# A hybrid block on one core: constants, modulation, norm, gates, lead and mixers in one program instead of six

## The reference

```python
c_act = silu(c)
mod = c_act @ ada_w + ada_b                       # 6 parts of 1024
sh_mix, sc_mix, gt_mix, sh_ffn, sc_ffn, gt_ffn = split(mod, 6)
h = rmsnorm(x, norm_mix) * (1 + sc_mix) + sh_mix
proj = h @ w_in                                   # all heads' q, k, v, gates
y = sum over branches sigmoid(merge_b) * mixer_b  # GLA 4 heads, mLSTM 4 heads, gated DeltaNet 8 heads
x = x + gt_mix * (y @ w_out)
h = rmsnorm(x, norm_ffn) * (1 + sc_ffn) + sh_ffn
x = x + gt_ffn * ((silu(gate(h)) * up(h)) @ w_ffn_down)
return rmsnorm(x, norm_final)
```

## Time and profile before

| | |
|---|---|
| median of 3 runs | 3057.71 us (3055.98 to 3058.48) |
| profiled execution | 3056.94 us, span 3055.2 us |
| granted TensorE clock, mean | 0.967 |
| before the mixers' program | 0 to 234.0 us |
| mixers: lead, 8 iterations, tail | 234.0 to about 2185 us |
| out projection, FFN | about 2185 to 3055 us |
| TensorE, VectorE, ScalarE, GpSimd busy | 93%, 60%, 32%, 15% |

### The profile page before, as it was taken

How to read it: one execution, slowest core, us unless ns; L and a number is a source line. 1 busy time by engine, 2 the same in 40 slices (tenths; PEclk the granted TensorE clock), 3 DMA queues, 4 the chain that set the end, 5 groups by cost and what they waited for, 6 DMA issues and landing times. The chain is left out here.

```text
span 3055.2 us, 46665 instructions
## 1 busy us (share of the span) xinstructions
PE 2839.0 (93%) x17688; PEld 2515.8 (82%) x17688; DVE 1821.3 (60%) x3548; ACT 972.1 (32%) x2191; POOL 456.0 (15%) x363
## 2 busy tenths in 40 slices
PE   7689999999999999999999999997398999999998
PEld 7378888898898898898898898896397888888887
DVE  0414686676667667666666656657545655566655
ACT  0304336336436535434434434422212000000002
POOL 1000003003003002100000000001103434443431
PEclk9969999999999999999999999998699999999999
DMA  4532112111111111111111111113611111111111
GB/s 128 166 112 50 32 25 54 32 25 53 35 25 39 36 32 35 44 35 33 47 33 30 51 32 30 51 39 90 186 29 56 48 49 42 56 49 49 49 56 56
DMA packets 251430, 161.73 MB, mean 53 GB/s; under 512 B 26971, under 2 KB 244931, under 8 KB 251205
## 3 DMA queue, kind: packets, MB, share of 16 engines
q1 hardware_dynamic: 251206, 158.74, 18.2%
HBM read 141.93 MB, written 16.79 MB: 52 GB/s over the span
## 5 line engine op out<-in xcount | busy, mean ns | idle before, releaser
L418 PE MATMUL bank<-wB_hi,h_hi 128*128 128x256 f32 x1088 | 317.2, 292 | 11.8 <-ACT conv_in L875 7.0
L418 PE MATMUL bank<-wA_hi,h_hi 128*128 128x256 f32 x1088 | 316.7, 291 | 9.5 <-ACT conv_in L875 3.0
L418 PE MATMUL bank<-wA_lo,h_hi 128*128 128x256 f32 x1088 | 317.4, 292 | 0.0
L418 PE MATMUL bank<-wB_lo,h_hi 128*128 128x256 f32 x1088 | 317.4, 292 | 0.0
L418 PE MATMUL bank<-wA_hi,h_lo 128*128 128x256 f32 x1088 | 316.4, 291 | 0.0
L418 PE MATMUL bank<-wB_hi,h_lo 128*128 128x256 f32 x1088 | 316.1, 291 | 0.0
L426 PE MATMUL bank<-h_hi,wA_hi 128*128 128x512 f32 x672 | 268.3, 399 | 16.1 <-PEq L103 15.6
L426 PE MATMUL bank<-h_hi,wB_lo 128*128 128x512 f32 x672 | 269.0, 400 | 0.0
L426 PE MATMUL bank<-h_hi,wA_lo 128*128 128x512 f32 x672 | 268.8, 400 | 0.0
L426 PE MATMUL bank<-h_hi,wB_hi 128*128 128x512 f32 x672 | 268.4, 399 | 0.2
L426 PE MATMUL bank<-h_lo,wA_hi 128*128 128x512 f32 x672 | 268.0, 399 | 0.0
(11 more groups left out here) (369 smaller groups left out, 6292.2 us busy)
## 6 DMA issues: line engine op xcount, KB each, us to landing
w_raw<-in_w_in_dram SPq DMA_DIRECT2D x96, 512.0 KB, 3.9
ada_ring<-in_ada_w_dram SPq DMA_DIRECT2D x24, 1024.0 KB, 5.6
w_raw<-in_w_ffn_up_dram SPq DMA_DIRECT2D x44, 512.0 KB, 3.8
w_raw<-in_w_ffn_down_dram SPq DMA_DIRECT2D x22, 512.0 KB, 3.6
y_scratch<-ybuf SPq DMA_DIRECT2D x64, 128.0 KB, 1.9
x_rows<-in_x_dram SPq DMA_DIRECT2D x8, 512.0 KB, 6.8
w_raw<-in_w_in_dram SPq DMA_DIRECT2D x16, 256.0 KB, 3.0
y_scratch<-ybuf SPq DMA_DIRECT2D x64, 64.0 KB, 1.6
```

The source lines that it names most:

```text
L418: mm = nc.tensor.matmul(bank[:, n_out:n_out + n1 - n0], (h_hi, h_lo)[hp][:, k, t * P:t * P + P], buf[wp][:, k, n0:n1], start=(s == 0), sto ...
```

## The change

All of sections 1 to 6 become one program, the mixers' one, without a barrier. The prologue (`constants_pool`, `prologue_sp`, `prologue_pe`, `prologue_act`, `prologue_dve`) is called at the head of each engine's list. x is loaded first and transposed before the modulation, which is then only eight pieces (shift and scale of the mixers' norm). The gates' work is cut into pieces that hang on beats of the lead (`lead_pe`, `lead_act`, `lead_dve`), and the lead has LB = 52 beats in place of 42, as the small projection is its first two units. The other four parts (gate of the mixers; shift, scale and gate of the FFN) are no longer matrix-vector matmuls: in each of the eight P1, VectorE accumulates half a part over eight slices of ada_w (`mod_dve`), and TensorE sums over the partitions with a column of ones (`mod_pe`). Buffers are laid over each other (`rows_region`, `feat_region`; the modulation ring over the weight buffers), and MAX_SEMS goes from 120 to 150. Later code is the same but for shifted counts of semaphores, and shifted lines: L1098 to L1100 of before are L1128 to L1130, L1085 is L1115.

```diff
+    def prologue_sp(sp):
+        for lo, n, v in ((0, 48, ada_b), (48, 8, norm_mix), (56, 8, norm_ffn), (64, 8, c[0])):
+            sp.dma_start(vec_rows[lo:lo + n, :], v.rearrange("(k p) -> k p", p=P)).then_inc(sem("vec_in"), 16)
+        sp.dma_start(conv_rows, gdn_conv.rearrange("j (k p) -> (j k) p", p=P)).then_inc(sem("vec_in"), 16)
+        for t in range(NT):
+            sp.dma_start(x_rows[:, t], x[t * P:t * P + P, :]).then_inc(sem(f"rows_in{t}"), 16)
+        for m in range(ADA_SLOTS):
+            ada_load(sp, m)
...
+    def prologue_act(act, step):
+        A = nc.scalar.activation
+
+        def x_norm(t):
+            act.wait_ge(sem(f"rows_in{t}"), 16)
+            step(A(sq_out, x_rows[:, t], ACT.Square, accum_out=ss_x[:, t:t + 1]))
+            step(A(ss_x[:, t:t + 1], ss_x[:, t:t + 1], ACT.Ln, scale=1.0 / D, bias=eps[:]))
+            step(A(rstd_x[:, t:t + 1], ss_x[:, t:t + 1], ACT.Exp, scale=-0.5), "x_rstd")
...
+        for t in range(4):
+            x_norm(t)
+        for t in range(4, NT):
+            x_evict(act, step, 2 * (t - 4))
+            x_norm(t)
...
+    def lead_act(act, step, b):
+        A = nc.scalar.activation
+        if b == 13:
+            act.wait_ge(sem("lead_dve"), LEAD_DVE["pre_cap"])
+            step(A(capped, capped, ACT.Tanh, scale=1.0 / ML_CAP), "lead_act")
+        elif b == 15:
+            act.wait_ge(sem("lead_dve"), LEAD_DVE["pre_exp"])
+            step(A(exp_g, exp_g, ACT.Abs))
+            step(A(exp_g, exp_g, ACT.Exp, scale=-1.0))
+            step(A(exp_g, exp_g, ACT.Ln, bias=1.0), "lead_act")
...
+    MOD_AT = [6 + 4 * k for k in range(KT)]
+    MOD_SUM_AT = (43, 46)
...
+    def mod_dve(dve, step, i, r):
+        part, half, as_row = mod_part(i)
+        if r in MOD_AT:
+            k = MOD_AT.index(r)
+            dve.wait_ge(sem(f"mod_in{k % 2}"), 16 * (mod_loads(k % 2, i) + k // 2 + 1))
+            if k == 0:
+                if i:
+                    dve.wait_ge(sem("g_sc"), NT * i)
+                step(dve.tensor_scalar(mod_acc, mod_ring[:, 0], c_act[:, 0:1], None, ALU.mult), "mod_acc")
+            else:
+                step(dve.scalar_tensor_tensor(mod_acc, mod_ring[:, k % 2], c_act[:, k:k + 1], mod_acc, ALU.mult,
+                                              ALU.add), "mod_acc")
...
     N_IT = GDN_H
     B1, B2, PAIR, CHUNK2, TAIL = 80, 42, 20, 5, 50
-    BEATS = B2 + N_IT * (B1 + B2) - B2 + TAIL
+    LB = 52
+    BEATS = LB + N_IT * (B1 + B2) - B2 + TAIL
...
+    units.extend((None, "small", half, -1, 0) for half in range(2))
     add_gdn(-1)
...
         def _(act):
             step = Steps(act, "act_step")
             nc.scalar.preload_act_table_set("natural_log_exp_and_others")
+            prologue_act(act, step)
             for b in range(BEATS):
                 i, r1, r2 = place(b)
+                if i < 0:
+                    lead_act(act, step, b)
...
         def _(dve):
             step = Steps(dve, "dve_step")
+            prologue_dve(dve, step)
             for b in range(BEATS):
                 i, r1, r2 = place(b)
+                if i < 0:
+                    lead_dve(dve, step, b)
...
                 if r1 is not None:
                     gdn_dve(dve, step, i, *divmod(r1, PAIR))
                     head_dve(dve, step, i, r1)
+                    mod_dve(dve, step, i, r1)
```

More of the change, by code:

```diff
@@ L214, in _build @@
[L214 to L240, removed]
-        else:
-            for i in range(ADA_W // P):
-                for k in range(KT):
-                    mm = nc.tensor.matmul(bank[:, i:i + 1], ada_ring[:, slot, k, i * P:i * P + P], c_act[:, k:k + 1],
-                                          start=(k == 0), stop=(k == KT - 1))
-        mm.then_inc(sem("ada_up"), 1)
@@ new lines, in ada_load, with ada_pe @@
+    def ada_load(sp, m):
+        part, j = ADA[m]
+        if m >= ADA_SLOTS:
+            sp.wait_ge(sem("ada_up"), m - ADA_SLOTS + 1)
+        o = part * D + j * ADA_W
+        sp.dma_start(ada_ring[m % ADA_SLOTS][:], ada_v[:, :, o:o + ADA_W]).then_inc(sem(f"ada_in{m % ADA_SLOTS}"), 16)
+    def ada_pe(pe, m):
+        slot, bank = m % ADA_SLOTS, banks[6 + m % 2]
+        pe.wait_ge(sem(f"ada_in{slot}"), 16 * (m // ADA_SLOTS + 1))
+        if m >= 2:
+            pe.wait_ge(sem("ada_out"), m - 1)
+        for i in range(ADA_W // P):
+            for k in range(KT):
+                mm = nc.tensor.matmul(bank[:, i:i + 1], ada_ring[slot][:, k, i * P:i * P + P], c_act[:, k:k + 1],
+                                      start=(k == 0), stop=(k == KT - 1))
+        mm.then_inc(sem("ada_up"), 1)
@@ new lines, in mod_stores, with mod_pe @@
+    def mod_stores(i):
+        return sum(mod_part(n)[2] for n in range(i))
+    def mod_pe(pe, i, r):
+        part, half, as_row = mod_part(i)
+        if r == MOD_SUM_AT[0]:
+            pe.wait_ge(sem("mod_acc"), KT * (i + 1))
+            if as_row:
+                mm = nc.tensor.matmul(M[5][0:1, 256:512], ones[:, 0:1], mod_acc[:, 0:256], start=True, stop=True)
+            else:
+                for q in range(4):
+                    mm = nc.tensor.matmul(M[5][:, 256 + q:257 + q], mod_acc[:, q * P:q * P + P], ones[:, 0:1],
+                                          start=True, stop=True)
+            mm.then_inc(sem("mod_sum"), 1)
+        elif as_row and r == MOD_SUM_AT[1]:
+            pe.wait_ge(sem("mod_row"), 2 * mod_stores(i) + 1)
+            nc.tensor.matmul(M[5][0:1, 256:512], ones[:, 0:1], mod_acc[:, 256:512], start=True, stop=True) \
+                .then_inc(sem("mod_sum"), 1)
@@ L846, in fill_unit @@
         if s0 == 0:
-            if first_unit[g] == u and g:
-                pe.wait_ge(sem("w_lo"), 4 * g)
+            if kind != "small" and first_unit[g] == u:
+                pe.wait_ge(sem("w_lo"), 4 * (g + 1))
             if u >= 2:
                 pe.wait_ge(sem(f"proj_read{u % 2}"), u // 2)
+        if kind == "small":
+            for s in range(s0, s1):
+                if s == 0:
+                    pe.wait_ge(sem("c_lo"), 1)
+                if s % 3 == 0:
+                    pe.wait_ge(sem("h_lo"), h_order(s // 3, n) + 1)
+                mm = feature_major(G[u % 2], n, C_W, 0, [s], SMALL)
+            if s1 == 3 * KT:
+                mm.then_inc(sem(f"proj{u % 2}"), 1)
+            return
         buf = (A_W, B_W)[g % 2]
@@ L1191, in head_pe @@
                 pe.wait_ge(sem("g2_in"), 16 * (i + 1))
+                for u in range(2):
+                    pe.wait_ge(sem(f"proj_read{u}"), 1)
             if 4 * i + n:
@@ L1519, in _build @@
     split_at = {}
-    for g in range(1, len(groups)):
-        b0 = after[g - 2] if g >= 2 else 0
+    for g in range(len(groups)):
+        b0 = after[g - 2] if g >= 2 else 8 * g
         split_at.setdefault(b0, []).append((g, 0))
         split_at.setdefault(b0 + 2, []).append((g, 1))
-    load_at = {0: [(1, 0), (1, 1)]}
+    load_at = {}
     for b, gs in split_at.items():
```

793 lines of the change are left out of this document (385 added, 408 removed).

## The result

The changed kernel takes 3289.55 us (median of 4 runs, 3285.18 to 3293.14), the kernel before 3058.1 (4 runs, 3055.98 to 3060.81). The ratio is 1.0756, with a 95% interval of 1.0737 to 1.0774: slower by 7.6%. The forecast was 3225, in a range of 3110 to 3330.

The account below looks back on a forecast made before the run. TensorE, busy 93% of the span, was taken to set the mixers' pace. 3056.9 −127 (front) +16 (modulation) +124 (P1 loads) +103 (P2 loads) +52 (clock) = 3225 us, range 3110 to 3330.

Parts of the forecast that it names:

- before the first P1: Sections ahead of iteration 0: its P1 starts at 172.3 instead of 299.5, a gain of 127 us.
- modulation's work in the P1: Eight new VectorE operations and TensorE's sums per P1, mostly covered: 2 us per iteration, +16 us.
- loads, TensorE idle in P1: Table loads at the norms of the chunk-pair boundaries stall TensorE 15.5 us per P1, +124 us for eight.
- loads, TensorE idle in P2: 22 table loads per P2 make TensorE 13.5 us late in GLA, 14 in mLSTM: +95 us for seven.
- loads, rest of the last head: Table loads in the last head's P2 delay TensorE: +8 us.
- clock: TensorE's new waits in P1 and P2 lower its granted clock: +52 us, bounds 0 to 155.
- first norm's step: At a P1 pair boundary, two loads make L1058, the matmul that takes rhs, 2.1 us late.
- second norm's step: At a P1 pair boundary, loads delay L1085, the masked product and then TensorE's L1040, by 2.5 us.
- last pair's first norm: In each P1, one last first norm beyond the three boundaries stalls TensorE by 2 us.
- hand-made shift: ScalarE's P2 rows shifted by the loads, idle times taken back, to see which matmul waits: +95 us for seven.
- one fall in three waits: Some 56 P1 and 35 P2 waits, a third taken to draw a clock fall costing 1.7 us: +52 us.
- B: Rival: the loads hide in ScalarE's free time in P1 and P2, giving 2950 us; chance 0.09.
- rule of the greedy longest run: Load placement would keep the set holding Exp and Ln: three loads in all, 2950 us; no chance of its own.

Follow-up runs that it names:

- e1: The changed kernel plus one preload of the set holding Exp and Ln, directly behind the lead's Tanh: 2936.04 us, ratio 0.9596.
- e2: The kernel before plus one Tanh of 128x1 behind the preload of its mixers' program: 3415.96 us, ratio 1.1173.
- e3: e1 with a Tanh of 128x1 at each P1's start and a preload of the joint set at each P2's start: 3107.37 us.
- e11: e1 with six ScalarE copies of 128x256 between Square and Ln of each GLA and mLSTM chunk norm in the P2: 3061.99 us.
- e12: The changed kernel with 16 unused TensorE matmuls of 128x128 ahead of the wait for rhs in each pair: 3263.0 us.
- e5: e1 with six ScalarE copies of 128x256 between Square and Ln of each of the 64 delta-rule norms: 3118.35 us.
- e4: e1 with a Tanh of 128x1 at each P2's start and a preload of the joint set at each P1's start: 3104.21 us.
- e7: e5 with the six copies only at the first norm of each pair: 3021.45 us, ratio 0.9875.
- e10: e5 with the six copies only at the second norm of each pair: 3021.23 us, ratio 0.9872.

## Why the prediction held, and which terms were off

The result lies inside the range and on the side forecast, 65 us above the likeliest value. The mechanism was right: e1 and e2 show that the table loads make all of the loss. Term by term, against the spans' stretches:

| term | predicted | measured |
|---|---|---|
| before the first P1 | −127 | −126.4 (299.5 to 173.0) |
| modulation's work in the P1 | +16 | +8 (e1's P1 against before's) |
| loads, TensorE idle in P1 | +124 | +94 (114.1 against e1's 20.4) |
| loads, TensorE idle in P2 | +95 | +108 (152.3 against 43.9) |
| loads, rest of the last head | +8 | +18 (115.2 against e1's 97.5) |
| clock | +52 | +133 (busy time: 61.7 in P1, 71.7 in P2) |

The measured column adds up to 234 of the 236 between the spans (e1's P2 and last head are not quite those of before); the predicted one to 168. The rows "in P1" do not cover quite the same norms: the 124 has the last pair's first norm in it, and the measured 94 has not (see P1).

**The front** was right to 1 us in the sum, and that is in part luck. The first matmul of the small projection starts at 81.02, where the sum has 88, and from there to the first P1 it takes 92 us where the sum has 84: two errors of 7 and 8 us cancel.

```profile
81.02 0.63 PE L178 MATMUL bank<-h_hi,wC_hi 128*40 128x512 f32 x1
```

The same front, three loads shorter, ends between 165.2 and 170.0 in the traces of e1 and e3 to e11, and in e12, which has the three loads, at 181.1.

**The table loads.** That the order showed 344, and that each costs 1.28 and no more, both held (64 loads of L1129, all 1283 ns). The Trainium skill, "ScalarE: Activation LUTs", section "What ACT_TABLE_LOAD costs", adds a drain of 1.38 to each switch: no run here shows it. The next activation starts 0.01 behind the load, and copies of the same length cost the same (e5 against e3).

**P1.** The first norm's step was right in place and size: 2.1 predicted at the matmul that takes rhs, 1.97 to 2.2 measured. The second norm's step named the wrong matmul. I followed ScalarE's list behind the norm to L1085 and from there to the masked product, as that had the least slack in the earlier trace rows. But between the norm and L1085 stands L877 (L905 after), the copy out of a projection bank, and the projection has only two banks. The kernel before shows that this copy had no slack either; ScalarE's row and TensorE's at the boundary of the earlier trace rows:

```profile
619.63 0.38 ACT L877 ACTIVATE vg<-bank 128x256 f32<-128x256 f32 x1
```

```profile
620.07 0.39 PE L418 MATMUL bank<-wA_hi,h_hi 128*128 128x256 f32 x1
```

The copy ends at 620.01, the projection goes on at 620.07, 2 us ahead of L1040, so TensorE comes for that bank first. The size, 2.5 against 2.4 on average (57.0 in 24 waits), was near since both hang on the same shift of 2.56. The 48 waits of the P1 windows add up to 106 us, where three boundaries of 4.5 in eight heads give 108. The idle time grows by 94 only, since the short waits that TensorE had at the masked product and ahead of it shrink from 13 us in e1 to 5. The last pair's first norm, predicted at 2, added 9 us over seven heads (it stands in the P2 windows: 13.2 at the rhs matmul against 3.9 in e1) and about 2 in the last. So 124 stands against some 105.

**P2.** Without those 9 us the measured 108 is 99, and e4, with loads in the P2 only, has 94 of idle time over e1: the 95 of the hand-made shift was right. In the last head it was 8 against some 16. Its P2, which has the gather of y in place of a projection, I had scaled from the others instead of reading.

**The clock** is the term that was mis-sized, 52 against 133. I took one fall in three waits, at 1.7 us each, from the earlier trace rows: 32 us for the 56 waits of the P1 and 20 for the 35 of the P2, where 62 and 72 were measured. In the P1 "one in three" was wrong. Of the waits that stand alone, e7's of 2.1 to 2.4 cost 0.85 each in longer matmuls (20.4 over the 24 in its P1) and e10's of 2.8 cost 1.4 (34.1 over 24), where a third of 1.7 is 0.57. Where both stand at one boundary, some 10 us apart, they cost 2.6 in the changed kernel (61.7 over 24) and 2.9 in e5. The boundary shown above cost more than the average, over 5 (half of ten us). In the P2 it was the size of the waits as well: I had taken all for waits of some 2.7, and TensorE waits 7.8, 3.3 and 4.0 in the first (rows above) and 6.3, 5.7, 3.4 and 2.5 in the first mLSTM P2. The longer matmuls there cost 10 us a head, where under 3 was forecast. Partly for this a GLA head took 283 to 292 us from clear to clear instead of 272 to 282. I had the upper end (155) from the same rows, and it would have been the better value.

**The rivals.** That the loads hide in ScalarE's idle two thirds (B) needed the matmuls to have slack; e7 shows they have none. Its other premise, that a load waits for no operand and so can fill ScalarE's waits, came from the earlier trace rows and does not hold everywhere. In the P2 loads begin only when the wait ahead of their activation is over:

```profile
2401.45 1.28 ACT L1415 ACT_TABLE_LOAD   x1 [1.79 <-DVE rs L1443]
```

The 32 loads of this line stand behind 43.7 us of such waits, the 17 of L1502 behind 24.6. Still, part of the loads hide: 335 loads are 430 us on ScalarE, and TensorE lost 220 to them in idle time. The rule of the greedy longest run (the Trainium skill, "ScalarE activation tables: per-element evaluation and per-set limits", section "Table sets in the compiler and the runtime") did not hold for this program: the loads alternate from the Tanh on, and one preload behind it ends that (e1).

## What to carry to other kernels

When programs are merged, count ScalarE's table loads in the compiled order before anything else: a single function from another set can leave every later change between two functions with a load, and a preload of the joint set behind it takes them away (353 us for one line here, 2936 against before's 3058). A busy share of 32% says nothing on whether 1.28 us more is hidden; what says it is the slack of the instruction that waits for the result, and every copy out of a PSUM bank that is queued behind it. And a wait of TensorE of 2 us can cost more than its length (32 of them in e7, 85 us above e1): read the busy time of the same matmuls, which grows when the clock falls.

## What was not expected of the hardware

Idle time of TensorE could be exchanged for useless matmuls at a gain: 512 of them made e7 faster by 18 us and the changed kernel by 27, with the clock of e7's P1 back at 1.00. And the loss was far from proportional to the time put on ScalarE: 1.3 us per norm cost 57 us in all, 2.67 us cost 182. In the P1, 69 of the 182 were the same matmuls at a lower clock, and 8 of the 57.
